# Seven half products in one FFN: one more pair sum on VectorE in place of a transfer, two-part loads, another order of the low halves

## What is computed

```python
def swiglu(x, w_gate, w_up, w_down):
    return (jax.nn.silu(x @ w_gate) * (x @ w_up)) @ w_down      # 1024 -> 2816 -> 1024
...
    h = h + gate * (p[i] @ w_ple_proj[i])                       # "ple" stage, 8 column blocks
h = h + 0.5 * swiglu(rmsnorm(h, norm_ffn1[i]), ...)             # the seven-product FFN, i = 1
```

## Time and profile before

| what | value |
|---|---|
| median of 3 runs | 3342.22 us |
| the profiled execution, its own time | 3343.81 us |
| its span in the trace | 3342.5 us |
| mean granted clock of TensorE | 0.992 |
| TensorE busy over the span | 3212.2 us (96%) |
| VectorE busy over the span | 1635.1 us (49%) |
| first product of the seven-product stage | 1100.22 us |
| first matmul of the down projection | 1347.54 us |
| idle of TensorE within the ple stage, longest | 7.91 us, ended by the low half of a weight tile |

### The profile page before, as it was taken

One profiled execution on the slowest core, in us unless ns is written; L12 is line 12 of the kernel. 1 busy time (PEld: TensorE's weight loads), 2 busy tenths in 40 slices (PEclk: granted clock), 3 DMA queues, 4 the chain that ended last, 5 costly groups with the idle time before them and its releaser, 6 DMA issues. The chain is left out here.

```text
span 3342.5 us, 49081 instructions
## 1 busy us (share of the span) xinstructions
PE 3212.2 (96%) x21088; PEld 2500.5 (75%) x21088; DVE 1635.1 (49%) x2492; ACT 1123.1 (34%) x1764; POOL 344.1 (10%) x409
## 2 busy tenths in 40 slices
PE   9999999999998999999999999988999999989988
PEld 7888887888887899788788888768877888524422
DVE  5443557554435878543654434686458544301112
ACT  4222226432224444422732223553345323200001
POOL 1000131200001111000210000301011301100000
PEclk9999999999999999999999999989999999999999
DMA  4223441122224687233222223301010233899998
GB/s 144 100 89 96 151 129 39 51 89 101 85 95 135 180 209 197 87 110 108 83 89 101 101 79 104 102 32 49 3 65 20 95 97 115 337 428 426 424 427 345
DMA packets 72312, 477.74 MB, mean 143 GB/s; under 512 B 9760, under 2 KB 11424, under 8 KB 42144
## 3 DMA queue, kind: packets, MB, share of 16 engines
q1 hardware_dynamic: 65760, 457.30, 36.9%
q0 software_dynamic: 6336, 17.30, 2.9%
HBM read 461.46 MB, written 2.10 MB: 139 GB/s over the span
## 5 line engine op out<-in xcount | busy, mean ns | idle before, releaser
L645 DVE TENSOR_TENSOR w_lo<-slot,w_hi 128x2048 fp32r<-128x2048 f32 (+4 forms) x221 | 436.8, 1976 | 298.4 <-ACT w_hi L636 296.3
L636 ACT ACTIVATE w_hi<-slot 128x2048 fp32r<-128x2048 f32 (+4 forms) x221 | 364.1, 1647 | 326.3 <-PE bank L176 318.1
L174 PE MATMUL bank<-xa,w_hi 128*128 128x512 f32 x1016 | 398.3, 392 | 1.7 <-DVE w_lo L3550 1.7
L175 PE MATMUL bank<-xa,w_hi 128*128 128x512 f32 x1016 | 395.5, 389 | 0.0
L176 PE MATMUL bank<-xa,w_lo 128*128 128x512 f32 x1016 | 395.4, 389 | 0.0
L174 PE MATMUL bank<-xb,w_hi 128*128 128x512 f32 x832 | 325.9, 392 | 9.1 <-DVE w_lo L645 9.1
L176 PE MATMUL bank<-xb,w_lo 128*128 128x512 f32 x832 | 324.7, 390 | 0.0
L175 PE MATMUL bank<-xb,w_hi 128*128 128x512 f32 x832 | 324.6, 390 | 0.0
L174 PEld LDWEIGHTS bank<-xa,w_hi 128*128 128x128 f32 x1016 | 190.7, 188 | 48.8 <-issue 5.2
L175 PEld LDWEIGHTS bank<-xa,w_hi 128*128 128x128 f32 x1016 | 190.7, 188 | 40.2 <-issue 1.0
L176 PEld LDWEIGHTS bank<-xa,w_lo 128*128 128x128 f32 x1016 | 190.7, 188 | 39.7
(11 more groups left out here) (555 smaller groups left out, 5916.5 us busy)
## 6 DMA issues: line engine op xcount, KB each, us to landing
slot<-in_w_gu SPq DMA_DIRECT2D x65, 1024.0 KB, 4.8
slot<-in_exp_gate SPq DMA_DIRECT2D x25, 2048.0 KB, 14.4
slot<-in_exp_up SPq DMA_DIRECT2D x24, 2048.0 KB, 15.0
slot<-in_exp_down SPq DMA_DIRECT2D x24, 2048.0 KB, 15.8
slot<-in_w_dn SPq DMA_DIRECT2D x64, 704.0 KB, 4.0
raw<-in_w_seven SPq DMA_DIRECT2D x22, 1280.0 KB, 7.2
slot<-in_w_gate SPq DMA_DIRECT2D x24, 768.0 KB, 4.3
xe<-in_exp_up SPq DMA_DIRECT2D x8, 2048.0 KB, 13.2
```

The lines of the kernel that those rows point to most:

```text
L174: e.matmul(out, w[0], x[0], start=(j == 0), stop=False)
L175: e.matmul(out, w[0], x[1], start=False, stop=False)
L636: act.e.activation(part(k, b)[0], slot(k, b), ACT.Copy).then_inc(L.up("w_hi", b))
L645: dve.e.tensor_tensor(lo, slot(k, b), hi.bitcast(F32), ALU.subtract).then_inc(L.up("w_lo", b))
```

## The change

- The second accumulating transfer and the buffer `pairs` go. The sum for product 6 is now added by VectorE into product 6's ring slot (`dve_comb_sum(…, 6, …)`); the low half of 6 overwrites it and so comes after the sum for 3.
- The stored weights lose the block that filled `pairs`: 3584 instead of 4096 numbers a row and m.
- SP loads each raw buffer in two parts: the 1024 numbers that POOL accumulates on, once low half 7 of m - 3 is made, then the other 1536, once low half 4 is made. The loads of m = 0 come ahead of the first ple tile in SP's order, and those of m = 1 ahead of the fourth, instead of both ahead of the fifth.
- Products run as 1, 5 of m = 0; 1, 5 of m = 1; the other five of m = 0; the other five of m = 1; then as before.
- In the ple stage, low halves 1 and 5 of m = 0 are made at i = 6 after h, those of m = 1 at i = 7 between the scaling and the multiply.
- VectorE's order in a period is as the diff shows; ScalarE's is unchanged from m = 1 on.
- Signs: two `scalar_tensor_tensor` of x combinations become `tensor_tensor`, and `two_more` subtracts.

```diff
 def sp_raw(k, b):
-    k.sp.wait_ge(*k.led.at(*free))
-    k.sp.e.dma_start(k.sv.raw[i], k.order[b][0][:, 0:2560])...
-    k.sp.e.dma_start(k.sv.pairs[i], k.order[b][0][:, 2560:3072])...
+    sp.wait_ge(*L.at(*frees[0]))
+    sp.e.dma_start(k.sv.raw[i][:, 1536:2560], k.order[b][0][:, 1536:2560]).then_inc(L.up(f"base_in{i}", b, by=16, also=[("w_base", b)]), 16)
+    sp.wait_ge(*L.at(*frees[1]))
+    sp.e.dma_start(k.sv.raw[i][:, 0:1536], k.order[b][0][:, 0:1536]).then_inc(L.up(f"raw_in{i}", b, by=16, also=[("w_in", b)]), 16)
...
-        if b == k.first["ple0"] + 4:
+        if b == k.first["ple0"]:
             sp_raw(k, k.first[f"gu{SEVEN_FFN}"])
+        if b == k.first["ple0"] + 3:
             sp_raw(k, k.first[f"gu{SEVEN_FFN}"] + 1)
...
+SEVEN_TURNS = [(p, m) for m in (0, 1) for p in (1, 5)] + [(p, m) for m in (0, 1) for p in SEVEN_ORDER[2:]] + [
+    (p, m) for m in range(2, FF) for p in SEVEN_ORDER]
...
+def dve_comb_sum(k, f, p, m):
+    dve, L, s, b = k.dve, k.led, seven_turn(p, m), k.first[f"gu{f}"] + m
     dve.wait_ge(*L.at(*seven_free(k, f, s)))
+    if p == 6:
+        dve.wait_ge(*L.at("w_sum", b))
+        dve.wait_ge(*L.at("w_in", b))
+        one, other = seven_raw(k, 5, m), seven_raw(k, 1, m)
+    else:
+        dve.wait_ge(*L.at("comb_sum", f, 6, m))
+        one, other = seven_slot(k, seven_turn(6, m))[3], seven_raw(k, 2, m)
+    dve.e.tensor_tensor(seven_slot(k, s)[3], one, other, ALU.add).then_inc(L.up("comb_sum", f, p, m))
...
 def pool_comb(k, f, m):
-    pool.wait_ge(*L.at("w_in", b))
-    pool.e.dma_start(k.sv.raw[m % 3][:, 1536:2560], k.order[b][0][:, 3072:4096], accum_op=ALU.add).then_inc(
+    pool.wait_ge(*L.at("w_base", b))
+    pool.e.dma_start(k.sv.raw[m % 3][:, 1536:2560], k.order[b][0][:, 2560:3584], accum_op=ALU.add).then_inc(
...
-    pool.wait_ge(*L.at("w_sum", b))
-    pool.e.dma_start(k.sv.pairs[m % 3], seven_raw(k, 5, m), accum_op=ALU.add)...
...
 (dve_seven)
-    dve_comb_sum(k, f, 0)
-    for p in (7, 3, 4):
+    dve_comb(k, f, 2, 0)
+    dve_comb_sum(k, f, 6, 0)
+    dve_comb(k, f, 7, 0)
+    dve_comb_sum(k, f, 3, 0)
+    for p in (6, 3, 4):
         dve_comb(k, f, p, 0)
+    dve_root(k, nm)
     for m in range(FF + 1):
+        if m and m + 1 < FF:
+            dve_comb(k, f, 1, m + 1)
+            dve_comb(k, f, 5, m + 1)
         if m:
             ends(m - 1)
-        if m + 1 < FF:
-            dve_comb(k, f, 1, m + 1)
-            dve_comb(k, f, 5, m + 1)
...
         if m:
             hidden(m - 1)
...
         gate_left(m)
         if m + 1 < FF:
             dve_comb(k, f, 2, m + 1)
-            dve_comb(k, f, 6, m + 1)
+            dve_comb_sum(k, f, 6, m + 1)
         two_more(m)
         if m + 1 < FF:
             dve_comb(k, f, 7, m + 1)
...
         rest(m)
         up_right(m)
         if m + 1 < FF:
-            dve_comb_sum(k, f, m + 1)
+            dve_comb_sum(k, f, 3, m + 1)
+            dve_comb(k, f, 6, m + 1)
             dve_comb(k, f, 3, m + 1)
             dve_comb(k, f, 4, m + 1)
...
 (act_seven)
+    act_comb(k, f, 2, 0)
+    first_part(0)
+    for p in (6, 7, 3, 4):
+        act_comb(k, f, p, 0)
+    act_root(k, nm, k.rstd_last)
...
 (act_ple)
-        if layer == 0 and i == KT - 1:
-            for p in (1, 5, 2, 6):
-                act_comb(k, SEVEN_FFN, p, 0)
...
+            if i >= KT - 2:
+                for p in (1, 5):
+                    act_comb(k, SEVEN_FFN, p, i - KT + 2)
...
 (pool_program)
-    for m in range(FF):
-        if m == 2:
-            pool_norm(k, "n4")
-        pool_comb(k, SEVEN_FFN, m)
+    pool_comb(k, SEVEN_FFN, 0)
+    pool_comb(k, SEVEN_FFN, 1)
+    pool_norm(k, "n4")
+    for m in range(2, FF):
+        pool_comb(k, SEVEN_FFN, m)
```

More of the change, by code:

```diff
@@ L276, in plan_seven @@
     assert b.at <= a.at
-    m.raw = [a.buf(5 * 512, "raw7") for _ in range(2)]
+    m.raw = [a.buf(5 * 512, "raw7") for _ in range(2)][::-1]
     b = area(a.at - 5120, 5120)
     early = [b.buf(512, "hid7_hi", F32R) for _ in range(10)]
-    m.hid = [(hi, lo) for hi, lo in zip(early[5:] + early[:5] + late, hid_lo)]
+    m.hid = [(hi, lo) for hi, lo in zip(early + late, hid_lo)]
     a = area(slots + 1536, 2560)
@@ L543, in plan_weights @@
             m = b - gu
-            k.raw_of[b] = (m % 3, ("comb_lo", SEVEN_FFN, seven_turn(4, m - 3)) if m > 2 else ("w_lo", gu - 1) if m == 2 else ("down", 1, 7))
+            k.raw_of[b] = (m % 3, [("comb_lo", SEVEN_FFN, seven_turn(p, m - 3)) if m > 2 else (("swiglu", 1, FF - 1), ("down", 1, 7), ("w_lo", gu - 1))[m]
+                                   for p in (7, 4)])
             continue
@@ L600, in sp_raw @@
 def sp_raw(k, b):
-    i, free = k.raw_of[b]
-    k.sp.wait_ge(*k.led.at(*free))
-    k.sp.e.dma_start(k.sv.raw[i], k.order[b][0][:, 0:2560]).then_inc(k.led.up(f"raw_in{i}", b, by=16), 16)
-    k.sp.e.dma_start(k.sv.pairs[i], k.order[b][0][:, 2560:3072]).then_inc(k.led.up(f"raw_in{i}", f"{b}", by=16, also=[("w_in", b)]), 16)
+    sp, L = k.sp, k.led
+    i, frees = k.raw_of[b]
+    sp.wait_ge(*L.at(*frees[0]))
+    sp.e.dma_start(k.sv.raw[i][:, 1536:2560], k.order[b][0][:, 1536:2560]).then_inc(L.up(f"base_in{i}", b, by=16, also=[("w_base", b)]), 16)
+    sp.wait_ge(*L.at(*frees[1]))
+    sp.e.dma_start(k.sv.raw[i][:, 0:1536], k.order[b][0][:, 0:1536]).then_inc(L.up(f"raw_in{i}", b, by=16, also=[("w_in", b)]), 16)
 def sp_weights(k, upto):
@@ L733, in seven_raw @@
 def seven_raw(k, p, m):
-    return k.sv.pairs[m % 3] if p == 6 else k.sv.raw[m % 3][:, SEVEN_RAW[p]:SEVEN_RAW[p] + 512]
+    return k.sv.raw[m % 3][:, SEVEN_RAW[p]:SEVEN_RAW[p] + 512]
+SEVEN_TURNS = [(p, m) for m in (0, 1) for p in (1, 5)] + [(p, m) for m in (0, 1) for p in SEVEN_ORDER[2:]] + [
+    (p, m) for m in range(2, FF) for p in SEVEN_ORDER]
 def seven_turn(p, m):
-    return 7 * m + SEVEN_ORDER.index(p)
+    return SEVEN_TURNS.index((p, m))
 def seven_slot(k, s):
@@ L774, in product @@
         last.then_inc(L.up("seven", f, s))
-    for m in range(FF):
[L777 to L780, removed]
+    for p, m in SEVEN_TURNS:
+        product(p, m)
+        if m == 0 and p == 6:
+            pe_norm(k, nm)
 def act_comb(k, f, p, m):
@@ L847, in dve_seven_x @@
         dve.wait_ge(*L.at("x7_diff", nm, j))
-        e.scalar_tensor_tensor(out=low[:, 1024:1280], in0=low[:, 1280:1536], scalar=-1.0, in1=high[:, 1024:1280], op0=ALU.mult,
-                               op1=ALU.subtract).then_inc(L.up("x6_diff", nm, j))
+        e.tensor_tensor(low[:, 1024:1280], low[:, 1280:1536], high[:, 1024:1280], ALU.add).then_inc(L.up("x6_diff", nm, j))
         dve.wait_ge(*L.at("x6_diff", nm, j))
-        e.scalar_tensor_tensor(out=low[:, 1536:1792], in0=low[:, 1024:1280], scalar=-1.0, in1=low[:, 512:768], op0=ALU.mult,
-                               op1=ALU.subtract).then_inc(L.up("x4_diff", nm, j))
+        e.tensor_tensor(low[:, 1536:1792], low[:, 1024:1280], low[:, 512:768], ALU.subtract).then_inc(L.up("x4_diff", nm, j))
         dve.wait_ge(*L.at("x23_hi", nm, j))
@@ L892, in silu, with first_part @@
         e.activation(gates, gates, ACT.Silu).then_inc(L.up("silu", f, m))
-    for p in (7, 3, 4):
[L895 to L899, removed]
+    def first_part(m):
         act.wait_ge(*L.at("seven", f, seven_turn(1, m)))
@@ L903, in act_seven @@
         e.activation(sv.first, k.banks.of("one", f, m)[:, 0:256], ACT.Copy).then_inc(L.up("first_part", f, m))
-        if more:
+    act_comb(k, f, 2, 0)
[3 more added lines that the diff above has]
+    act_root(k, nm, k.rstd_last)
+    for m in range(FF):
+        more = m + 1 < FF
+        if m and more:
+            act_comb(k, f, 1, m + 1)
+        if m:
+            first_part(m)
+        if m and more:
             act_comb(k, f, 5, m + 1)
@@ L955, in two_more @@
             dve.wait_ge(*L.at("rest", f, m - 1))
-        e.tensor_tensor(sv.two, k.banks.of("six", f, m)[:, 0:256], sv.first, ALU.add).then_inc(L.up("two_more", f, m))
+        e.tensor_tensor(sv.two, sv.first, k.banks.of("six", f, m)[:, 0:256], ALU.subtract).then_inc(L.up("two_more", f, m))
     def rest(m):
@@ L1750, in dve_ple @@
         e.tensor_tensor(g, k.banks.of("ple_gate", layer, i)[:, :], k.rstd, ALU.mult).then_inc(L.up("ple_scaled", layer, i))
+        if layer == 0 and i == KT - 1:
+            for p in (1, 5):
+                dve_comb(k, SEVEN_FFN, p, 1)
         dve.wait_ge(*L.at("ple_sigmoid", layer, i))
@@ L1758, in dve_ple @@
         if layer == 0:
+            if i == KT - 2:
+                for p in (1, 5):
+                    dve_comb(k, SEVEN_FFN, p, 0)
             dve_seven_x(k, nx, i)
```

28 lines of the change are left out of this document (7 added, 21 removed).

## The result

| | kernel before | changed kernel |
|---|---|---|
| median | 3342.41 us (3338.76 to 3345.60, 10 runs) | 3350.02 us (3345.99 to 3352.78, 10 runs) |
| profiled execution, its span | 3343.81, 3342.5 us | 3347.70, 3346.4 us |
| VectorE busy | 1635.1 us | 1655.3 us |
| low half 4 of m = 1 | 1123.56 | 1119.80 |
| low half 4 of m = 21 | 1338.14 | 1344.57 |

The ratio is 1.0019, with an interval of 1.0011 to 1.0028: the change costs 6.4 us (3.7 to 9.4), where 5.5 were forecast. The ratio is an estimate from all runs and not the quotient of the medians, which differ by 7.6 us. The place to read the cost is the end of the stage: the first matmul of the down projection comes 6.43 us later, and so does the last low half 4, so all of it arose before.

The account below looks back on a forecast made before the run. The seven-product stage was taken as bound by the chain load, first accumulation, second accumulation. 4.3 us gained up to its low half 4 of m = 1 and 9.8 lost over 20 periods gave +5.5: 3347.7 against 3342.22, range 3333 to 3358.

Parts of the forecast that it names:

- (a): Seven-product stage: without the second transfer and with loads in two parts, ScalarE's five transfer waits, 30.0 us together, go.
- (b): VectorE's period in the seven-product stage: two new waits, 0.80 and 0.98, make it 11.22 us; +9.8 us over 20 periods.
- (c): Ple stage: ScalarE's 10.87 us wait for POOL goes, 2 x 1.08 comes back where POOL and VectorE coincide; gain 8.7 us.
- (d): Low halves around i = 6, 7 of the ple stage: gain 2.4 us before block 7's scaling, loss 1.7 at i = 7.
- (e): Start of the seven-product stage, up to low half 4 of m = 1: 19.0 us against 13.9, loss 5.1.
- Rival 1: Seven-product stage: VectorE's new waits don't appear, TensorE paces at 10.08; 3325 us; any gain needs under 10.51; chance 0.11.
- Rival 2: Seven-product stage: each period's wait slows TensorE's clock, the period grows to 11.5 or 11.6; 3355 us, chance 0.06.
- Rival 3: Seven-product stage: the transfers still hold it, waits of 5 to 6 us come back; +15, 3362 us, chance 0.02.
- Rival 4: Ple stage and start: they gain nothing, held by low halves or moved loads; the 4.3 go, 3352 us, chance 0.07.

Follow-up runs that it names:

- both, and the start: Kernel "both" with low halves 1, 5 of m = 1 after h, norm matmul and reciprocal later, high half 7 of m = 0 before 6: 3322.64 us, 0.9944.
- POOL waits again: Changed kernel with raw loads of m = 0, 1 ahead of the fifth ple tile and POOL awaiting each of those transfers' end: 3353.35 us, 1.0035.
- both: Changed kernel with low halves 1 and 5 between `ends` and `hidden`, and ScalarE's high half 7 ahead of 6: 3330.15 us, ratio 0.9969.

## Why the prediction was right

**(a)** Held. No wait for `pairs` or `raw` on ScalarE; that the second transfer caused the old 1.29 a period is shown by the kernel without it, where the period falls to VectorE's own 9.44 and then to TensorE's 10.08. The timing of the loads is worth nothing, nor is their splitting (two runs).

**(b)** Held, and it is the sign of the result. Walked 11.22, measured 11.24; idle 0.70 and 0.88 at the two places named. Each wait was removed alone by order and gave back the price it was put down with (0.82 for 0.80, 0.98 for 0.98). The added sum costs next to nothing: with both waits gone and TensorE not yet pacing, the sums of "both, and the start" are 9.45 to 9.48 apart, where they were 9.44 before. Over the 20 periods: (1344.57 - 1119.80) - 214.58 = +10.2, where the sum had +9.8. One reading of it failed in part: TensorE's wait before product 6 (0.93 to 1.00, for some 1.1) is in the last 15 periods only.

**(c)** Right in cause, and close in size. From the add to h of block 0 to that of block 4 the changed kernel gains 8.9 us, for 8.7, and so does the kernel before without the second transfer; both have VectorE's coincidence with POOL (1.51 for an x difference, as in the earlier trace rows). The cause is shown by the run that brings the wait back.

**(d)** The loss of 1.7 at i = 7 is in the trace: scaling to multiply takes 3.11 us, the walk's very number. The gain was 2.1 and not 2.4, since the low halves of m = 0 cost 0.3 at their new place. Both are too small for the times. The swapped signs cost nothing: from the add to h of block 7 to the last low half of its x it is 4.84 us before and 4.82 after.

**(e)** From low half 2 to low half 4 of m = 1 it took 1119.80 - 1100.06 = 19.7 for the 19.0 walked, a loss of 5.8 for 5.1. The walk holds up to product 6 (4.67 in, for 4.7). Then the product took 2.7 for 2.5 and the norm's two matmuls 1.9 for 1.2, so the reciprocal started 10.0 in and not 9.2; all later steps keep that distance within 0.1. This depends on the start's clock: in the second execution the reciprocal started 8.0 in.

Together (c) to (e) make 3.8 instead of 4.3, and 0.3 of the 3.8 was there at block 0, ahead of the change. At the down projection the two traces of the changed kernel are 6.4 and 4.5 us behind the one of before. That 5.5 fell between them is right by its terms; that it came so near is in part luck.

**Rival 1** (TensorE paces, 3325) was false here for the reason given, and came true at its own condition: with both waits gone the sums are 10.08 apart. The limit of 10.51 that it gives for any gain has a sign wrong: with 4.3 us from the start it is 10.73 + 4.3/20 = 10.95. The runs lie at 10.42 and below or at 11.23, so they don't tell the two apart. **Rival 2** (the clock, 3355) did not come. The wait of 1.00 us before product 6 is followed by starts 0.19 and then 0.12 apart and by granted clock 1.00; from 1134.7 us on none of the 536 matmuls of line 778 took over 0.36 us. Behind the two longer waits of the periods (3.24 and 2.34) the clock did fall, for some 3.5 us each. The Trainium skill (TensorE: Matmul & The Clock Gate, HAM oscillation) warns of a fall back to half clock in every turn of a loop that waits, with a transfer of some 3 to 5 us as its example; in this trace that holds for the two waits above 2 us and for none of the periods' waits of 0.93 to 1.00. Their length alone doesn't decide it. Where POOL waits again, a wait of 3.23 us that ends at 1121.39 is followed by starts 0.12 apart and granted clock 1.00 up to 1127; in "both", one of 2.00 that ends at 1126.30 is followed, after a few at 0.12, by starts 0.21 apart. **Rival 3** is excluded by (a). **Rival 4** was wrong: 3.8 of the 4.3 arrived, or 3.5 without the head start.

**Open.** The three kernels with other orders ended the stage 15.8, 18.9 and 20.0 us earlier than the changed kernel in their traces, but by ratios gained 11, 17 and 17. Of this some 2 us can be the changed kernel's start (its second trace ended 1.9 earlier), and the intervals are 3 us to each side. By medians, each less its own kernel before, the gains are 14, 18 and 18. So the gap is no larger than what the way of summing up the runs makes, and no run shows that it is real.

## What to carry to other kernels

Before low halves, sums or the like are moved ahead of another step "because their inputs are there", ask what they covered where they stood: here two subtractions hid the round trip VectorE, ScalarE, VectorE, and its price, two handovers less one instruction, could be read from the trace of before. When work is moved onto an engine, walk a whole period of all engines' fixed orders with start-to-start prices: a step that waits for a late result (high half 6) delays the one behind it that doesn't need it, and swapping the two costs nothing. And gains on an engine count only down to the next one's pace: 0.82 and 0.98 gave 1.16 together.

## What was not expected of the hardware

Two executions of the same changed kernel differ by 1.9 us at the end of this stage, and the source is how fast TensorE goes after one wait: product 6 of m = 0 has starts 0.12 apart in one and 0.21 in the other, and the norm's two matmuls take 1.0 and 1.9 us, behind waits of 0.93 and 0.94 us and a product with starts 0.21 apart in both. That is as large as the effect of moving two instructions, and more runs of a kernel help less against it than a trace read at the place in question.
